# Retention with its gates and state update in one stage; stacked outer products; norm weights at eviction

## The reference

```python
h = x + Mix(RMSNorm(x));  h = h + PEER(RMSNorm(h));  y = RMSNorm_final(h)
# Mix: one input projection, then two branches
#  A: gated DeltaNet, 4 heads of 128 x 128
#  B: retention, 4 heads, DK 128, DV 256
def step(S, xs):                       # retention, per chunk and head
    o = inner_c + qd_c @ S             # inner = (q k^T * D) v
    S = S * gC + kd_c^T @ v_c
o_b = rmsnorm(o_b, gn_b) * silu(gate_b)        # per head; likewise o_a with gn_a
merged = sigmoid(sel_a) * (o_a @ w_br_a) + sigmoid(sel_b) * (o_b @ w_br_b)
m = merged @ w_out
```

## Time and profile before

| what | value |
|---|---|
| median of 3 runs | 2587.88 us |
| lowest, highest | 2581.29, 2588.79 us |
| the profiled execution | 2593.21 us |
| its span, first to last instruction | 2591.4 us |
| mean granted TensorE clock | 0.925 |
| busy over the span: PE, DVE, ACT, POOL | 75%, 50%, 23%, 48% |
| stage starts (us): gate A, proj_b, rotation, retention, gate B | 504.6, 543.5, 663.9, 701.9, 744.8 |
| branches, output projection, experts | 807.0, 894.4, about 991 |

### The profile page before, as it was taken

How to read it: one execution, slowest core, us unless ns; L and a number is a source line. 1 busy time by engine, 2 the same in 40 slices (tenths; PEclk the granted TensorE clock), 3 DMA queues, 4 the chain that set the end, 5 groups by cost and what they waited for, 6 DMA issues and landing times.

```text
span 2591.4 us, 25137 instructions
## 1 busy us (share of the span) xinstructions
PE 1951.0 (75%) x8728; PEld 1216.7 (47%) x8728; DVE 1308.6 (50%) x2801; ACT 604.6 (23%) x1273; POOL 1256.7 (48%) x1084
## 2 busy tenths in 40 slices
PE   5988698479876787858776776777777777677778
PEld 4987698479756787833222222222222222222222
DVE  2144533221643416964565666565666665665541
ACT  4223122222133233222211122111221221211211
POOL 0020120100110003667777777777777777777774
PEclk9998799779876897979999999999999999999999
DMA  4221020261104224899999999999999999999997
GB/s 124 91 64 39 25 67 21 65 204 49 49 33 172 92 71 148 304 336 352 353 370 359 374 371 350 353 361 364 356 377 351 360 368 352 361 382 358 367 366 274
DMA packets 246986, 636.91 MB, mean 246 GB/s; under 512 B 20927, under 2 KB 106239, under 8 KB 246482
## 3 DMA queue, kind: packets, MB, share of 16 engines
q0 software_dynamic: 149760, 545.33, 56.6%
q1 hardware_dynamic: 97114, 90.18, 11.0%
HBM read 617.59 MB, written 17.93 MB: 245 GB/s over the span
## 4 chain that ended last, share of the span: by engine, by line
POOL 26%; DMA 13%; PE 10%; issue 9%; DVE 2%; another core or an unknown queue 0%; ACT 0%; DVEq 0%; POOLq 0%
POOL v_row L1716 13%; POOL ex_u_row L1711 13%; DMA v_row<-in_peer_v,ex_eidx 13%; PE ps L1767 9%; DVE ex_u_row L1925 1%; DMA wq_raw<-in_peer_wq 0%; DVE ex_w_lo L1859 0%; PE ps L543 0%; PE ps L545 0%; PE ps L544 0%; DMA ex_u_row<-in_peer_u,ex_eidx 0%; ACT ex_w_hi L1794 0%; DVE ex_hot L1910 0%; DVE ex_res L1912 0%
## 5 line engine op out<-in xcount | busy, mean ns | idle before, releaser
L1767 PE MATMUL ps<-v_row,ex_spread 128*128 128x512 f32 (+1 forms) x2080 | 1048.8, 633 | 410.5 <-DMA v_row<-in_peer_v,ex_eidx 327.7
L1925 DVE CUSTOM_DVE_ANT_0 ex_u_row<-ex_u_row,x_ffn 128x1024 f32<-128x1024 f32 x512 | 626.1, 1228 | 551.6 <-DMA ex_u_row<-in_peer_u,ex_eidx 495.2
L1767 PEld LDWEIGHTS ps<-v_row,ex_spread 128*128 128x128 f32 (+1 forms) x2080 | 364.1, 193 | 1077.7 <-DMA v_row<-in_peer_v,ex_eidx 673.4
L1716 POOL DMA_INDIRECT v_row<-in_peer_v,ex_eidx x512 | 585.4, 1143 | 198.3 <-issue 127.8
L1711 POOL DMA_INDIRECT ex_u_row<-in_peer_u,ex_eidx x512 | 562.8, 1099 | 214.8 <-issue 149.6
L1811 ACT ACTIVATE ex_spread<-square,ret_tables 128x128 f32<-128x128 f32 (+1 forms) x520 | 184.8, 393 | 752.6 <-PE ps L1767 380.0
L335 POOL TENSOR_TENSOR x_ffn<-norm_xn,norm_gains_row 128x1024 f32<-128x1024 f32 (+1 forms) x5 | 14.0, 2810 | 217.5 <-ACT norm_xn L290 217.5
L593 POOL TENSOR_TENSOR dp_w_lo<-dp_w_raw,dp_w_hi 128x1024 fp32r<-128x1024 f32 x10 | 24.0, 2404 | 173.9 <-ACT dp_w_hi L619 173.9
L1805 ACT ACTIVATE ret_tables<-ret_tables 128x16 f32<-128x16 f32 (+1 forms) x33 | 7.1, 215 | 414.6 <-DVE ret_tables L1925 239.7
L543 PE MATMUL ps<-proj_b_whi,x_lo 128*128 128x256 f32 (+1 forms) x320 | 91.1, 285 | 9.7 <-DVE proj_b_wlo L484 9.7
L593 POOL TENSOR_TENSOR rope_w_lo<-rope_w_raw,rope_w_hi 128x1024 fp32r<-128x1024 f32 x4 | 10.8, 2712 | 168.1 <-ACT rope_w_hi L619 168.1
(11 more groups left out here) (397 smaller groups left out, 3446.4 us busy)
## 6 DMA issues: line engine op xcount, KB each, us to landing
first_raw<-in_w_in SPq DMA_DIRECT2D x8, 1024.0 KB, 7.7
wq_raw<-in_peer_wq SPq DMA_DIRECT2D x16, 512.0 KB
ex_u_row<-in_peer_u,ex_eidx POOLq DMA_INDIRECT x512
v_row<-in_peer_v,ex_eidx POOLq DMA_INDIRECT x512
dp_w_raw<-in_w_in SPq DMA_DIRECT2D x10, 512.0 KB
proj_a_raw<-in_w_in SPq DMA_DIRECT2D x4, 1024.0 KB, 5.0
proj_b_raw<-in_w_in SPq DMA_DIRECT2D x4, 1024.0 KB, 5.2
S_sample<-in_state_ret SPq DMA_DIRECT2D x1, 4096.0 KB, 23.6
```

The source lines that it names most:

```text
L1716: pool.indirect_dma_start(v_row[:, n % RING, :], None, a["peer_v"][0], bass.IndirectOffsetOnAxis(ap=index_of(n), axis=0)).then_inc(v_loade ...
L1767: ins = pe.matmul(k.pv[t % 2][0:r, c, :], spread[:, n % RING, 0:r], v_row[:, n % RING, c * 512:(c + 1) * 512], start=first, stop=last)
L1925: dve.tensor_tensor_reduce(u, u, x, 1.0, 0.0, ALU.mult, ALU.add, coef[:, n:n + 1]).then_inc(dotted, 1)
```

## The change

- Norm weights: `gn_a` and `gn_b` are loaded as columns in the constants phase (two more small loads and two small additions for a mask `whose8`), no longer broadcast in norm1; GpSimd's gate multiplies are gone, and `hi` and `lo` apply the weight as a scale per partition when they leave PSUM. For B the eight column blocks are turned in two groups of four, even and odd, so that each has one weight column.
- Outer products: keys and values of the 8 samples are stacked along the contraction (hi, hi, lo against hi, lo, hi at rows 0, 32, 64, zeros between), so that one float32r product of 72 rows takes the place of an fp32 one. A class `Stack` builds them: GpSimd clears, ScalarE copies twice, VectorE subtracts.
- Gate A builds its stacks at its own start, turns a tile before the outer products of every pair of samples, and keeps the other order. Rotation builds the stacks for B: the values first on every engine, the keys last.
- `retention` replaces `retention_prompt` and gate B. Samples come first (all 32 products with the state, before chunk 0), then chunks; tiles are gated in the order samples, 0, 1, 2, 3, each one chunk later. 16 units of outer products (two heads each) go through one PSUM bank, one after each head. Scores use one bank (before two).
- `stream` takes `then`, a load into its first buffer at its end; "branches" uses it for the first chunk of `w_out`. `merged` has its own buffer, `x_hi` and `x_lo` take the gated B output. `x_ffn`, `w_raw` and `v_row` move from the right side of the on-chip memory to the left.

```diff
+                if then is not None:
+                    sp.wait_ge(w_lo_done, FREE_RAW + 2 * sum(job.steps for job in jobs) - 1)
+                    sp.dma_start(raw[0][:, :, :], then).then_inc(then_loaded, 16)
+                    sp.wait_ge(then_loaded, 16)
...
+    def on_tensor(self, pe, n):
+
+        b, u = divmod(n, self.units)
         pe.wait_ge(self.masked, b + 1)
-        wait(pe, self.updated, b - 1)
-        for h in range(H):
-            ins = pe.matmul(self.bank(b, h), self.key_of[0:NS, b % 2, h * P:(h + 1) * P],
-                            self.values[0:NS, h * self.width:(h + 1) * self.width], start=True, stop=True)
+        wait(pe, self.updated, n - len(self.banks) + 1)
+        for j in range(self.per_bank):
+            h = u * self.per_bank + j
+            ins = pe.matmul(self.k.pb[self.banks[n % len(self.banks)]][:, j * self.width:(j + 1) * self.width],
+                            self.key_of[0:STACK, b % 2, h * P:(h + 1) * P],
+                            self.values[0:STACK, h * self.width:(h + 1) * self.width], start=True, stop=True)
         ins.then_inc(self.outer, 1)
...
+class Stack:
...
+    def on_gpsimd(self, pool):
+
+        pool.memset(self.rows[0:STACK, :].bitcast(F32), 0.0).then_inc(self.cleared, 1)
+
+    def on_scalar(self, act, src):
+
+        act.wait_ge(self.cleared, 1)
+        act.activation(self.rows[0:NS, :], src, ACT.Copy).then_inc(self.upper, 1)
+        act.activation(self.rows[self.second:self.second + NS, :], src, ACT.Copy).then_inc(self.upper, 1)
+
+    def on_vector(self, dve, src):
+
+        dve.wait_ge(self.upper, 2)
+        return dve.tensor_tensor(self.rows[self.lo_at:self.lo_at + NS, :], src, self.rows[0:NS, :].bitcast(F32), ALU.subtract)
...
+def retention(k, a, o, qk_b, v_b, kb_tok, S_sample, key_rows, value_rows, gate, hi, lo, early):
...
                 scores(0)
+                pe.wait_ge(sample_q, 1)
...
+                for h in range(H):
+                    for b in range(NS):
+                        ins = pe.matmul(r_ps(h)[0:NS], qm[:, h, b, :], S_sample[:, b, h, :], start=(b == 0), stop=(b == NS - 1))
+                ins.then_inc(sample_mm, 1)
                 for t in range(NCH):
...
+                        pe.matmul(o_ps(h), A[:, t % 2, h, :], v(t, h), start=not t, stop=True)
+                        ins = pe.matmul(s_ps(h), kb_tok[:, t, h * P:(h + 1) * P], v(t, h), start=True, stop=True)
+                        if h == H - 1:
+                            ins.then_inc(os_mm, 1)
+                        if t == 0 and h == 0:
+                            pe.wait_ge(dots_taken, 1)
+                        states.on_tensor(pe, H * t + h)
+                        if t and h == 1:
+                            turn(t - 1)
+                turn(NCH - 1)
+                turn(NCH)
...
                 for t in range(NCH):
                     if t + 1 < NCH:
-                        prep(t + 1)
+                        decayed(t + 1)
+                    for h in range(H - 1):
+                        states.on_vector(dve, H * t + h)
+                    if t:
+                        lower(t - 1)
                     dve.wait_ge(os_mm, t + 1)
...
+                    states.on_vector(dve, H * t + H - 1)
+                    scale(t)
+                scale(NCH)
+                lower(NCH - 1)
+                lower(NCH)
```

More of the change, by code:

```diff
@@ L61 @@
 TOPK = 16
+GROUP = 32
+STACK = 2 * GROUP + NS
 HP = 2 * PH
@@ L366, in stream @@
 @phase
-def stream(k, name, jobs, extra=(), first_raw=None):
+def stream(k, name, jobs, extra=(), first_raw=None, then=None):
     nc = k.nc
@@ L1179, in on_tensor @@
-    def on_tensor(self, pe, b):
-        pe.wait_ge(self.masked, b + 1)
-        wait(pe, self.updated, b - 1)
-        for h in range(H):
-            ins = pe.matmul(self.bank(b, h), self.key_of[0:NS, b % 2, h * P:(h + 1) * P],
-                            self.values[0:NS, h * self.width:(h + 1) * self.width], start=True, stop=True)
-        ins.then_inc(self.outer, 1)
-    def on_vector(self, dve, b):
-        dve.wait_ge(self.outer, b + 1)
-        for h in range(H):
-            ins = dve.scalar_tensor_tensor(self.S[:, b, h, :], self.S[:, b, h, :], self.decay(b, h), self.bank(b, h),
+        if b < NS:
+            wait(act, self.outer, self.units * (b - 1))
+            act.activation(self.key_of[0:STACK, b % 2, :], self.keys[0:STACK, :], ACT.Copy,
+                           scale=self.k.whose8[0:STACK, b:b + 1]).then_inc(self.masked, 1)
@@ L1193, in on_vector @@
+    def on_vector(self, dve, n):
+        b, u = divmod(n, self.units)
+        dve.wait_ge(self.outer, n + 1)
+        for j in range(self.per_bank):
+            h = u * self.per_bank + j
+            ins = dve.scalar_tensor_tensor(self.S[:, b, h, :], self.S[:, b, h, :], self.decay(b, h),
+                                           self.k.pb[self.banks[n % len(self.banks)]][:, j * self.width:(j + 1) * self.width],
                                            ALU.mult, ALU.add)
@@ L1291, in gate_and_turn @@
 @phase
-def gate_and_turn(k, a, name, o_tok, gate, gn, width, hi, lo, early, states):
+def gate_and_turn(k, a, o_tok, gate, hi, lo, early, S, keys, dv, decay, out):
     nc = k.nc
-    W = H * width
-    nb = W // 512
+    name, width = "gate_a", DK
     with ExitStack() as ctx:
@@ L1314, in _ @@
             def _(pool):
-                for t, r in enumerate(ROWS):
-                    pool.tensor_tensor(heads(gate, t, r), heads(gate, t, r),
-                                       gn[0:r, :].unsqueeze(1).to_broadcast([r, H, width]), ALU.mult).then_inc(gained, 1)
-                    if t == 0:
-                        side.on_gpsimd(pool)
+                key_stack.on_gpsimd(pool)
+                value_stack.on_gpsimd(pool)
             @block.vector
@@ L1479, in _ @@
             def _(sp):
+                begin(sp, early, early_loaded)
+                states.on_sync(sp)
                 sp.wait_ge(s_done, NCH)
@@ L1482, in _ @@
                 sp.wait_ge(stored, 16)
+                wait(sp, early_loaded, 16 * len(early))
             @block.tensor
@@ L1537, in _ @@
                 ins.then_inc(sample_q, 1)
+                dve.memset(ss[:, :, :], 0.0).then_inc(cleared, 1)
+                decayed(0)
+                dve.wait_ge(dots_mm, 1)
+                fence(dve, dve.tensor_copy(dots[:, :], k.pb[1][0:NS, 0:H]), dots_taken, 1)
+                t1 = sq[0:NS, :, :]
+                own.fence(dve.tensor_tensor(t1, heads(v_b[0:NS, NCH, :]), head_bc(dots[:, :], NS, DV_B), ALU.mult))
+                dve.wait_ge(sample_mm, 1)
+                for h in range(H):
+                    ins = dve.scalar_tensor_tensor(v_b[0:NS, NCH, h * DV_B:(h + 1) * DV_B], r_ps(h)[0:NS],
+                                                   float(gammas()[h]), t1[:, h, :], ALU.mult, ALU.add)
@@ new lines, in upper @@
+                def upper(j):
+                    t, r = ORDER[j], ROWS[ORDER[j]]
+                    for c in range(2):
+                        act.wait_ge(turned, 2 * j + c + 1)
+                        act.activation(hi[:, c:DC:2, t * P:t * P + r], turn_ps(c, r), ACT.Copy,
+                                       scale=k.gn_b[:, c:c + 1]).then_inc(hi_done, 1)
+                states.on_scalar(act, 0)
+                states.on_scalar(act, 1)
+                act.wait_ge(cleared, 1)
+                act.wait_ge(sample_out, 1)
```

390 lines of the change are left out of this document (207 added, 183 removed).

## The result

| | kernel before | changed kernel |
|---|---|---|
| median of the runs shown beside each other | 2587.2 us (2581.3 to 2588.8, 4 runs) | 2548.3 us (2546.8 to 2551.8, 4 runs) |
| ratio, 95% interval | 1 | 0.9858 (0.984 to 0.9875) |
| profiled execution: span | 2591.4 us | 2550.1 us |

A forecast was written before the change was run, and what follows sets the result against it. Experts, DMA engines 96% busy, fill the last 1431 of 2591 us and should only start earlier; chains and TensorE bound changed stages. -4.5 + 5.0 - 36.2 - 5.6 + 0.8 = -40.5 gives 2547 us, range 2538 to 2565.

The forecast's parts named there:

- Gate A: Gate A stage: cheaper stacked outer products shorten the period from 7.33 to 5.2 us, start plus 2.3; booked minus 4.5 us.
- The row that I called nearest: Gate A pricing: float32r products of 256 columns, one record each, 0.24 us apart at the low clock.
- Rotation: Rotation stage: VectorE starts 4.9 us late behind the value stack, transposes move 3.8, key copies add 1.2; plus 5.0 us.
- the plus 6: Rotation stage: plus 6 us instead of plus 5.0 if the transposes run at the low clock after the new gap.
- Fused stage: Retention and gate B merged: 68.9 us with the barrier, against 105.1 before; minus 36.2 us.
- The term of the rounds: Fused stage: three rounds of 11.4 us, 34.2 in all, TensorE stalling 1.9 a round for a unit's update.
- the low-clock rival: Fused stage at the low clock from its first round on: rounds 15.2 us, plus 16, so 2563 us; chance 0.16.
- Output projection: Output projection: early load of the first weight chunk brings its first product 3.3 us after the start; minus 5.6 us.
- Constants: Constants stage: two more DMA issues on SP and two small VectorE additions; plus 0.8 us.
- Float32r brings nothing: Gate A and fused rounds: float32r products cost as fp32 does, so 2559 us; chance 0.10.
- The gathers get slower: Experts stage: moved gather buffers cut the rate 2.8%, 1431 us grows by 40, the gain is gone; chance 0.04.
- The fusion is not what is gained: Fused stage: handovers over one bank stretch rounds to 14 us, plus 8, so 2555 us; no chance of its own.

The follow-up runs named there:

- the run with stacked products: Kernel before with norm weights applied at eviction and stacked float32r outer products in gates A and B, no fusion: 2568.6 us, ratio 0.9933.
- the kernel with the norm weights alone: Kernel before with only the norm weights applied as `hi` and `lo` are made, GpSimd's gate multiplies gone: 2579.5 us, ratio 0.9982.
- the padded run: Changed kernel with 1472 unused bytes a partition among the constants, shifting later tiles: 2551.4 us, ratio 0.9868; its fused stage took 65.5 us.

## Why the prediction was right, step by step

- **Gate A.** -3.3, not -4.5. The mechanism held (first update 13.5 us after the start, 13.8 forecast); the size of one term was off. A sample's four float32r products take 1.0 us, 0.21 to 0.24 apart and 0.36 to the next sample's, where I had booked 0.5: back to back, 128 columns cost at this clock what 256 do (the first eight records of 256 columns in gate B of the run with stacked products took 2.06 us, 0.21 apart after the first; the 2.75 shown there has a handover behind each pair). The row that I called nearest gave the spacing, and halving it for half the columns was the error. The period is 5.68, not 5.2.
- **Rotation.** +5.8 for +5.0, by terms that erred both ways. The transposes moved by 3.6 (3.8 forecast) and waited for VectorE, as forecast (1.77 us, shown above). But the side products ended later, too (34.5 us after the start, before 32.9), which the kernel with the norm weights alone shows without any late start; there the transposes moved by 1.4. The late start is thus worth 2.2 of the 3.6, and that the sum came out is in part luck. The transposes then ran at the low clock (4.4 us for 3.5), which stood in the prediction as the plus 6.
- **Fused stage.** 68.4 for 68.9. Sample phase 16.7 (17.5), first round 6.5 (6.05), rounds 33.9 (34.2), tail and barrier 11.3 (11.1). The term of the rounds is right by two errors: the same code at full clock makes them in 31.0, so I had put TensorE's stall (1.9 in each round, for 1.54, 1.56 and none) and the queue too high, and the low-clock rival, which I priced for the whole stage at 16, came true for some 3 us at two places. Against this rival stood that TensorE never idles over 2 us; it idled 1.54 and 2.00 ahead of the two dips, and 4.53 in the tail, which ran at 0.57. Why the clock falls at these two places and not in the padded run with the same stalls is open.
- **Output projection.** -6.1 for -5.6; first product 3.3 us after the start, as forecast. The run without the early load gives 5.7.
- **Constants.** +0.5 for +0.8.
- **What the sum left out.** The stages between the constants and the delta samples +1.3, which two profiles of the changed kernel differ by, too (471.5 and 470.1); the delta samples +1.9, of which the rate of the loads explains 1.2; `proj_b` -1.4 and branches -1.6, in which TensorE's clock rises at other times. They nearly cancel, which no step had foreseen: that the whole came within 2 us is in part luck.
- **The rivals.** "Float32r brings nothing" fell: undoing it costs 12.6 us in two stages. "The gathers get slower" fell. "The fusion is not what is gained" as I put it (rounds of 14) fell; but half of the stage's gain (18.0 of 36.7, and 1.5 of the clock) comes without fusion, which the prediction did not ask.

## What to carry to other kernels

Price a product by its record's spacing in a row of the same width at the same clock: here 128 columns came no closer together than 256 (0.21 us at the low clock). The weight loads of both came at that spacing, which fits the prediction's guess that they set it, but no run separates the two. Before fusing two chains, make each cheap by itself and measure: here that gave 18.0 of 36.7 us without touching the order. Compare the clock of each stretch before giving a difference to an edit: 1.5 us of the norm weights' 5.5 were the clock's. And in a fused loop put the update that frees a single bank ahead of long work on the same queue (5.0 us here, 2.1 of it by the order alone).

## What the runs showed of the hardware

- The rate of loads in 512-byte pieces changed with where they land: 347 GB/s with the states at 256 modulo 512, 290 at 320 and at 224; weights at 160 kept 348, so no one multiple at which all tiles are to start explains it. Adding or dropping a few constants moved every tile after them.
- Dense transposes raise and hold the granted clock as products do (0.21, then 0.11 us a record).
- A stage with no changed line took 83.5 to 88.7 us. Where TensorE's clock rose early, it ran out of weights sooner (9.7 us after the start, not 10.7), idled 3.8 us and came back slow (88.4 and 88.7); with a gap of 1.6 it kept its rate (83.5).
- The granted clock fell to 0.50 behind idle stretches of 1.54 and 2.00 us in six profiles, and not behind the same ones in a seventh (1.00 throughout).
- Chips differ by 45 us in the same kernel.
